# Softmax of both attentions: the inverse sum goes into the turning product instead of into the exponentials

## The chip, the cores and the metric

One NeuronCore of a Trainium2 chip runs the whole kernel. The metric is the device time of one execution in microseconds; lower is better. The kernel before has a median of 1913.64 us over three runs (1910.66 to 1914.75).

## What is computed

The reference is two layers of a hybrid backbone over 256 latent tokens and 256 context tokens of width 1024. The even layer mixes with a 2-D Fourier transform and an 8-head neighbourhood attention, then a dense SwiGLU; the odd layer has a 12-head attention with 3 key heads, an S5 recurrence, and a top-2-of-8 SwiGLU of experts. What matters here is the softmax of the two attentions, which is followed by a product with the values:

```python
s = jnp.einsum('bqhgd,bkhd->bhgqk', q_blk, k_all).astype(jnp.float32) * dh ** -0.5
p = jax.nn.softmax(s, axis=-1).astype(v_all.dtype)
return jnp.einsum('bhgqk,bkhd->bqhgd', p, v_all)
```

In the even layer latent queries see latent and context keys (512, with a bias and a mask on the latent ones) and context queries see context keys (256). In the odd layer only latent queries are used, over 512 keys. All of this is float32.

## The kernel before

The program is written by hand, engine by engine, with semaphores between them; each engine runs its own list in order. The stages follow one another: modulation and input projection of the even layer, turning of q and k, Fourier mixing, even attention (about 184 to 262 us), output product, dense layer, odd projection with S5 set-up, odd attention (about 788 to 848 us), output product, router, experts (from about 860 us to the end).

Both attentions use the same functions, one for each engine, over a list of steps: `EVEN_STEPS` has 16 (2 streams, latent then context, by 4 pairs of heads by 2 query tiles; 8 steps of 512 keys and 8 of 256), `ODD_STEPS` has 12 (6 pairs of heads by 2 query tiles, 512 keys). A step is 128 queries of two heads; the index i counts heads through both attentions, two a step, 56 in all.

For each head, in order:

- TensorE makes the scores, queries on partitions and keys along a row, into one of three PSUM banks (L681).
- DVE adds the bias in the even latent steps (L1627), which waits for POOL to have built that head's bias (`bias_ready`, POOL L2112 and L2128), and takes the negated maximum (L1632).
- ScalarE makes the exponential from PSUM into `prob[:, i % 3]` in SBUF, with the row sum beside it (L1236).
- DVE inverts the sum (L1637) and scales the exponentials by it in place (L1638).
- TensorE turns each 128x128 chunk of them into PSUM, bank 3 or 4 (L696): one transpose for each 128 keys, with the identity from the constants.
- ScalarE copies the turned chunks to `pT` in SBUF (L1246).
- TensorE multiplies them with the values, both heads of the step into bank 5 ("pv", L713).
- DVE copies that output to its place (L1646).

The order is a software pipeline that is written out. In round r TensorE issues the scores of step r, then (even layer) a modulation product of the next layer (`UNDER_ATTN`, L563), then pv of step r - 2, then the turn of step r - 1, then (odd layer) a piece of S5: output products (L940, L944), their turn (L953), the gating product (L964), and gate rows (L729). A gate row is four calls of `pe.matmul`, 128x128 by 128x128 against the identity; there are twelve rows, 48 calls. ScalarE in round r makes the exponentials of step r, then the copies of the turned chunks of step r - 1. DVE in round r makes the maxima of step r, then for each head the inverse and the scaling, then the o copy of step r - 2, then its piece of S5.

The waits that tie them: the exponential of head i waits for the turn of head i - 3 (`prob_turned`, L1235), since `prob` has three buffers; the scores of step r wait for the exponentials of step r - 1's first head (`exp_done`, L679); the turn of head i waits for its scaling (`prob_ready`, L692) and for the copy of head i - 2 (`pt_ready`, L694); pv waits for both copies (L707) and the o copy of the step before (L709).

During the even attention POOL builds the bias of the heads and tables of the odd layer's S5 in one sequence (L2112 to L2152). B is the large scratch tile of the mixing stages; in the even attention its columns 0 to 2047 held the Fourier input, and in the odd one its columns 3840 to 4863 held the S5 input `un`, which has been stored to memory by then.

Of the kernel before, what the change touches and what calls it, by code (L numbers as in the profile page):

```python
# [26 lines left out]
P = 128  # L27
# [119 lines left out]
def build(nc, a, out):  # L147
    ctx = ExitStack()
    with ctx:
        def sb(name, shape, dt=F32):  # L150
            return ctx.enter_context(nc.sbuf_tensor(name, shape, dt))

        def sem(name):
            return ctx.enter_context(nc.semaphore(name))

        bank = [ctx.enter_context(nc.psum_tensor(f"bank{i}", [P, 512], F32)) for i in range(8)]
# [9 lines left out]
        with ExitStack() as mixing:  # L166
            def mix(name, shape, dt=F32):
                return mixing.enter_context(nc.sbuf_tensor(name, shape, dt))
# [3 lines left out]
            B = mix("B", [P, FC * TOK])  # L172
# [33 lines left out]
        rinv = sb("rinv", [P, 4])  # L206

        ident = cst[:, C_ID:C_ID + P]
# [21 lines left out]
        prob = S[:, 1024:2560].rearrange("p (b n) -> p b n", b=3)  # L230
# [55 lines left out]
        def w_et(u, c):  # L286
# [30 lines left out]
        row_max, exp_done, prob_ready, prob_turned, pt_ready, o_psum, o_ready = (  # L317
            sem("row_max"), sem("exp_done"), sem("prob_ready"), sem("prob_turned"),
            sem("pt_ready"), sem("o_psum"), sem("o_ready"))
# [110 lines left out]

        qT, kT = hT[:, 0:4], hT[:, 4:8]

        def mod_bank(g):
            return bank[(0, 3, 7)[g]]

# [8 lines left out]
        def even_steps():  # L444
            steps = []
            for s in range(2):
                for p in range(NA_HEADS // 2):
                    for t in range(2):
                        q = [qT[x, p, (2 * s + t) * P:(2 * s + t + 1) * P] for x in HALVES2]
                        k = [kT[x, p, SEQ * s:] for x in HALVES2]  # L450
                        v = [[hn[:, 3, c, h * HD:(h + 1) * HD] for c in range(2 * s, 4)] for h in (2 * p, 2 * p + 1)]
                        steps.append((q, k, TOK - SEQ * s, v, p, s, t))
            return steps

        EVEN_STEPS = even_steps()
# [95 lines left out]
        def _(pe):  # L551
            def modulation(s):

                wait_slot(pe, S_MOD[s])
                g = [s < hi for _, hi in MOD_GROUPS].index(True)
                lo, hi = MOD_GROUPS[g]
                o = mod_bank(g)
                at = 30 - 2 * (s - lo)
                w = slot(S_MOD[s]).rearrange("p (k n) -> p k n", k=DC)
                for i in range(2):  # L560
                    for j in range(4):
                        c = 4 * i + j
                        mm = pe.matmul(o[32 * j:32 * j + 32, :], silc[:, c, at:at + 32], w[:, c, :],  # L563
                                       start=(s == lo and i == 0), stop=(s == hi - 1 and i == 1))
                mm.then_inc(mod_psum, 1)
# [105 lines left out]
            def attention(steps, j0):  # L671

                n = len(steps)
                for r in range(n + 2):
                    if r < n:
                        q, k, keys = steps[r][0:3]
                        i = 2 * (j0 + r)
                        if i >= 2:
                            pe.wait_ge(exp_done, i - 1)  # L679
                        for h in range(2):  # L680
                            pe.matmul(bank[(i + h) % 3][:, 0:keys], q[h], k[h], start=True, stop=True).then_inc(scores[h], 1)  # L681
                        if steps is EVEN_STEPS:
                            if r in UNDER_ATTN:
                                modulation(UNDER_ATTN[r])
                            if r == 0:
                                pe.wait_ge(four_o, 8)
                    if r >= 2:
                        pe_pv(steps[r - 2], j0 + r - 2)
                    if 1 <= r <= n:
                        for h in range(2):  # L690
                            i = 2 * (j0 + r - 1) + h
                            pe.wait_ge(prob_ready, i + 1)  # L692
                            if i >= 2:
                                pe.wait_ge(pt_ready, i - 1)  # L694
                            for c in range(steps[r - 1][2] // P):
                                mm = pe.transpose(bank[3 + i % 2][:, c * P:(c + 1) * P],  # L696
                                                  prob[:, i % 3, c * P:(c + 1) * P], ident)
                            mm.then_inc(prob_turned, 1)
                        if steps is EVEN_STEPS and r == ROW_AT + 1:
                            modulation_turn(2)  # L700
                    if steps is ODD_STEPS:
                        s5_step(r)

            def pe_pv(step, k):

                keys, v = step[2:4]
                pe.wait_ge(pt_ready, 2 * k + 2)  # L707
                if k >= 1:
                    pe.wait_ge(o_ready, k)  # L709
                o = bank[5][:, P * (k % 2):P * (k % 2) + P]  # L710
                for c in range(keys // P):
                    for h in range(2):
                        mm = pe.matmul(o[HALVES2[h], :], v[h][c], pT[:, k % 2, h, c * P:(c + 1) * P],  # L713
                                       start=(c == 0), stop=(c == keys // P - 1))
                        if c == keys // P - 1:
                            mm.then_inc(o_psum, 1)
# [277 lines left out]
            for t in range(2):  # L994
                for c in range(DC):
                    mm = pe.matmul(bank[2][:, 8 * t:8 * t + 8], hT[:, c, t * P:(t + 1) * P],
                                   vec[:, V_RW + 8 * c:V_RW + 8 * c + 8], start=(c == 0), stop=(c == DC - 1))
# [4 lines left out]
            for o, parts in ((0, [(tri, 0)]), (8, [(one, 0), (tri, 1)]), (16, [(one, 0), (one, 1)])):  # L1002
                for k, (m, t) in enumerate(parts):
                    mm = pe.matmul(bank[3][:, o:o + 8], m, sel[:, 8 * t:8 * t + 8], start=(k == 0),
                                   stop=(k == len(parts) - 1))
# [453 lines left out]
        def _(dve):  # L1459
            steps = [0]  # L1460
# [155 lines left out]
            def attention(steps, j0, oTv, c0):  # L1616
                n = len(steps)
                for r in range(n + 2):
                    if r < n:
                        keys, _, p, s, t = steps[r][2:7]  # L1620
                        for h in range(2):
                            i = 2 * (j0 + r) + h
                            sc = bank[i % 3]
                            dve.wait_ge(scores[h], j0 + r + 1)
                            if steps is EVEN_STEPS and s == 0:
                                dve.wait_ge(bias_ready, 2 * p + h + 1)
                                dve.tensor_tensor(sc[:, 0:SEQ], sc[:, 0:SEQ], bias[(2 * p + h) % 4][:, t * SEQ:(t + 1) * SEQ],  # L1627
                                                  ALU.add).then_inc(bias_used, 1)
                                dve.wait_ge(bias_used, i + 1)
                            if i >= 4:  # L1630
                                dve.wait_ge(exp_done, i - 3)
                            dve.tensor_reduce(nmax[:, i % 4:i % 4 + 1], sc[:, 0:keys], AX, ALU.max,  # L1632
                                              negate=True).then_inc(row_max, 1)
                        for h in range(2):
                            i = 2 * (j0 + r) + h
                            dve.wait_ge(exp_done, i + 1)
                            step(dve.reciprocal(rinv[:, i % 4:i % 4 + 1], rsum[:, i % 4:i % 4 + 1]))  # L1637
                            dve.tensor_scalar(prob[:, i % 3, 0:keys], prob[:, i % 3, 0:keys], rinv[:, i % 4:i % 4 + 1],  # L1638
                                              None, ALU.mult).then_inc(prob_ready, 1)
                        if steps is EVEN_STEPS and r == ROW_AT:  # L1640
                            modulation_row(2)
                    if r >= 2:
                        k = j0 + r - 2
                        p, s, t = steps[r - 2][4:7]
                        dve.wait_ge(o_psum, 2 * k + 2)
                        dve.tensor_copy(oTv[:, c0 + p, s * SEQ + t * P:s * SEQ + (t + 1) * P],  # L1646
                                        bank[5][:, P * (k % 2):P * (k % 2) + P]).then_inc(o_ready, 1)
                    if steps is ODD_STEPS:
                        s5_step(r)
# [24 lines left out]
            for u, what in enumerate(F_ORDER):  # L1674
                if u + AHEAD < F_UNITS:
                    split(u + AHEAD)
                if what[0] == "up" and what[2] == 1:
# [7 lines left out]
                    for f in range(2):  # L1685
                        c = (2 * n + f) % max(FG)
# [641 lines left out]
```

## Time and profile before

| | |
|---|---|
| Median of three runs | 1913.64 us (1910.66 to 1914.75) |
| The profiled execution | 1914.57 us, span 1912.7 us |
| Mean granted TensorE clock | 0.977 of full |
| TensorE busy | 1814.9 us, 95% |
| DVE, ScalarE, POOL busy | 66%, 52%, 16% |
| The chain that ended last | 90% TensorE, 3% DMA, 3% DVE, 2% POOL |
| DVE scaling L1638, 56 of them | 28.0 us for 40 of 512 columns, 8.0 us for 16 of 256 |
| TensorE turn L696, 192 records | 29.4 us |

The span is the time from the first to the last instruction of one profiled execution; the execution's own time is a little longer. A busy share is an average over stages with different limits, so the table says where time is spent and not what an edit is worth. A group of the timeline, such as eight matmul records, is given with its start and its length from the first start to the last end; matmul records overlap, since each lasts about 0.27 us from issue to landing while the next follows sooner.

### The profile page before, as it was taken

How to read it: one execution, taken by the hardware profiler on the slowest of the kernel's cores; microseconds unless marked ns; L12 is line 12 of the kernel's file. 1: busy time of each engine (PE TensorE's matmuls, PEld its weight loads, DVE VectorE, ACT ScalarE, POOL GpSimd, SP SyncE). 2: the span in 40 equal slices, each digit the busy share in tenths (PEclk: the TensorE clock that was granted, in tenths of full speed). 3: DMA queues.
4: the chain of work that ended last, by engine and by line, in shares of the span. 5: the costliest groups of instructions: out<-in, count | busy, mean ns of one | idle time of the engine just before them, and what ended most of it. 6: DMA issues, size and time to landing. Idle time of an engine off the chain costs nothing.

```text
span 1912.7 us, 25247 instructions
## 1 busy us (share of the span) xinstructions
PE 1814.9 (95%) x8938; PEld 1413.6 (74%) x8938; DVE 1265.6 (66%) x1329; ACT 1003.7 (52%) x1096; POOL 312.3 (16%) x584
## 2 busy tenths in 40 slices
PE   4999788999999989797999999999999999999998
PEld 2666444888888876465888888888888888888886
DVE  3243734442433234744998989989889898898997
ACT  3222423421312121363677767777777777776774
POOL 6887931011111124101000000000000000000000
PEclk8999899999999999897999999999999999999999
DMA  9788532122323151502799999999989999898994
GB/s 371 307 337 272 195 127 88 43 111 77 121 77 121 45 203 56 165 2 88 289 370 355 352 370 337 368 352 355 371 344 359 349 358 368 346 362 345 364 367 182
DMA packets 72374, 481.55 MB, mean 252 GB/s; under 512 B 8368, under 2 KB 11568, under 8 KB 17456
## 3 DMA queue, kind: packets, MB, share of 16 engines
q1 hardware_dynamic: 68720, 470.82, 64.5%
q0 software_dynamic: 2448, 7.61, 1.5%
q10 hardware_dynamic: 1136, 2.21, 0.4%
q8 instruction: 41, 0.67, 0.1%
q14 instruction: 29, 0.24, 0.0%
HBM read 473.29 MB, written 7.32 MB: 251 GB/s over the span
## 4 chain that ended last, share of the span: by engine, by line
PE 90%; DMA 3%; DVE 3%; POOL 2%; issue 1%; ACT 1%; SPq 0%; DVEq 0%; ACTq 0%; POOLq 0%
PE bank L1042 32%; PE bank L1056 16%; PE bank L775 12%; PE bank L745 4%; PE bank L804 3%; PE bank L792 3%; PE bank L625 3%; PE bank L840 2%; DMA ring<-in_ev_mod 2%; PE bank L563 2%; PE bank L1015 2%; PE bank L1025 1%; PE bank L713 1%; PE bank L605 1%; PE bank L696 1%
## 5 line engine op out<-in xcount | busy, mean ns | idle before, releaser
L1806 DVE TENSOR_TENSOR rest<-ring,WR 128x2048 fp32r<-128x2048 f32 x336 | 758.3, 2288 | 80.6 <-ACT WR L1373 80.1
L1373 ACT ACTIVATE WR<-ring 128x2048 fp32r<-128x2048 f32 x336 | 632.3, 1917 | 48.4 <-DMA ring<-in_experts 47.9
L1042 PE MATMUL bank<-WR,xer 128*128 128x512 f32 x1792 | 582.0, 397 | 0.8 <-DVE s5v L1967 0.8
L1042 PEld LDWEIGHTS bank<-WR,xer 128*128 128x128 f32 x1792 | 337.0, 188 | 70.3 <-issue 0.8
L1042 PE MATMUL bank<-rest,xer 128*128 128x512 f32 x896 | 349.5, 390 | 0.0
L1056 PE MATMUL bank<-WR,heTr 128*128 128x512 f32 x896 | 282.2, 392 | 0.0
L775 PE MATMUL bank<-hTr,WR 128*128 128x512 f32 x672 | 207.2, 390 | 0.0
L1056 PEld LDWEIGHTS bank<-WR,heTr 128*128 128x128 f32 x896 | 168.2, 188 | 34.6
L1042 PEld LDWEIGHTS bank<-rest,xer 128*128 128x128 f32 x896 | 169.1, 189 | 32.9
L1056 PE MATMUL bank<-rest,heTr 128*128 128x512 f32 x448 | 174.4, 389 | 0.0
L1658 DVE TENSOR_TENSOR rest<-ring,WR 128x2048 fp32r<-128x2048 f32 (+2 forms) x38 | 80.3, 2115 | 123.9 <-ACT WR L1298 123.6
L2232 POOL CAST gTe<-B 128x256 fp32r x8 | 3.2, 401 | 972.3 <-PE bank L1015 972.3
L775 PEld LDWEIGHTS bank<-hTr,WR 128*128 128x128 f32 x672 | 125.8, 188 | 25.9
L775 PE MATMUL bank<-hTr,rest 128*128 128x512 f32 x336 | 130.7, 389 | 0.0
L1394 ACT ACTIVATE sile<-bank 128x256 f32<-128x256 f32 x112 | 43.0, 384 | 161.5 <-PE bank L1042 161.5
L2008 POOL TENSOR_TENSOR X<-X,tmpf 128x512 f32<-128x512 f32 x32 | 52.6, 1671 | 321.0 <-DVE tmpf L1544 321.0
L1056 PEld LDWEIGHTS bank<-rest,heTr 128*128 128x128 f32 x448 | 84.2, 188 | 16.8
L1298 ACT ACTIVATE WR<-ring 128x2048 fp32r<-128x2048 f32 (+2 forms) x38 | 63.9, 1688 | 43.7 <-DMA ring<-in_ffn_up 43.7
L745 PE MATMUL bank<-ring,B 128*128 128x512 f32 x192 | 85.4, 602 | 0.9 <-issue 0.5
L563 PE MATMUL bank<-ring,rows 128*32 128x512 f32 x384 | 50.7, 648 | 25.1 <-DMA ring<-in_ev_mod 24.8
L775 PEld LDWEIGHTS bank<-hTr,rest 128*128 128x128 f32 x336 | 63.1, 188 | 13.2
L745 PEld LDWEIGHTS bank<-ring,B 128*128 128x128 f32 x192 | 36.6, 194 | 45.1 <-issue 44.3
(338 smaller groups left out, 2175.4 us busy)
## 6 DMA issues: line engine op xcount, KB each, us to landing
ring<-in_experts SPq DMA_DIRECT2D x336, 1024.0 KB, 4.8
ring<-in_ev_mod SPq DMA_DIRECT2D x24, 1024.0 KB, 9.0
ring<-in_od_mod SPq DMA_DIRECT2D x24, 1024.0 KB, 8.6
ring<-in_ffn_up SPq DMA_DIRECT2D x22, 1024.0 KB, 6.8
ring<-in_ffn_down SPq DMA_DIRECT2D x12, 768.0 KB, 5.1
ring<-in_ev_in SPq DMA_DIRECT2D x8, 1024.0 KB, 6.7
ring<-in_ev_out SPq DMA_DIRECT2D x4, 1024.0 KB, 8.5
ring<-in_od_out SPq DMA_DIRECT2D x4, 1024.0 KB, 13.5
```

What stands on the lines that cost most here:

```text
L563: mm = pe.matmul(o[32 * j:32 * j + 32, :], silc[:, c, at:at + 32], w[:, c, :], start=(s == lo and i == 0), stop=(s == hi - 1 and i == 1))
L625: mm = pe.matmul(bank[IN_BANK[j % 4]][:, :], h[i], w[k], start=(c == 0 and y == 0), stop=(c == DC - 1 and y == 2))
L745: mm = pe.matmul(bank[3 + b % 4][:, :], oTv[:, c, t * P:(t + 1) * P], w[:, c, :], start=(c == 0), stop=(c == DC - 1))
L775: mm = pe.matmul(bank[2 * m + f][:, :], w[i][:, c, f * P:(f + 1) * P], hTr[:, j, c, :], start=(c == 0 and x == 0), stop=(c == DC - 1 and x ...
L792: mm = pe.matmul(bank[t][:, :], gTr[:, i, c, t * P:(t + 1) * P], both[j][c // ks][:, c % ks, :], start=(c == 0 and x == 0), stop=(c == FG[ ...
L804: mm = pe.matmul(bank[t + 4][:, :], gTr[:, i, c, t * P:(t + 1) * P], w[j][:, k, :], start=(c == 0 and x == 0), stop=(c == FG[q] - 1 and x ...
L1042: mm = pe.matmul(bank[m % 2][:, :], xer[:, i, 4 * kh + k, :], w[j][:, 512 * k:512 * k + 512], start=(kh == 0 and k == 0 and x == 0), stop= ...
L1056: mm = pe.matmul(bank[4 + h][:, :], heTr[:, i, c, :], w[j][:, D * k + 512 * h:D * k + 512 * h + 512], start=(c == 0 and x == 0), stop=(c = ...
L1298: act.activation(part(0, h, n), ring[:, h % HALVES, 0:n], ACT.Copy).then_inc(split_hi, 1)
L1373: act.activation(part(0, h), ring[:, h % HALVES, :], ACT.Copy).then_inc(split_hi, 1)
L1658: dve.tensor_tensor(part(1, h, n), ring[:, h % HALVES, 0:n], part(0, h, n).bitcast(F32), ALU.subtract).then_inc(split_lo, 1)
L1806: dve.tensor_tensor(part(1, h), ring[:, h % HALVES, :], part(0, h).bitcast(F32), ALU.subtract).then_inc(split_lo, 1)
```

## The change

DVE no longer scales the exponentials. It writes the identity, scaled row by row by the inverse sums, into a 128x128 tile, one of three in turn; these stand in B at columns 0 to 383 in the even attention and 3840 to 4223 in the odd one. TensorE turns the unscaled exponentials by a product with that tile, so that turning and scaling are one product. DVE waits, before it writes the tile of head i, for the turn of head i - 3.

```diff
         qT, kT = hT[:, 0:4], hT[:, 4:8]
 
+        def inverse(steps, i):
+            return (B[:, P * (i % 3):P * (i % 3) + P] if steps is EVEN_STEPS else
+                    B[:, 3840 + P * (i % 3):3840 + P * (i % 3) + P])
+
...
                             for c in range(steps[r - 1][2] // P):
-                                mm = pe.transpose(bank[3 + i % 2][:, c * P:(c + 1) * P],
-                                                  prob[:, i % 3, c * P:(c + 1) * P], ident)
+                                mm = pe.matmul(bank[3 + i % 2][:, c * P:(c + 1) * P],
+                                               prob[:, i % 3, c * P:(c + 1) * P], inverse(steps, i),
+                                               start=True, stop=True)
                             mm.then_inc(prob_turned, 1)
...
                             step(dve.reciprocal(rinv[:, i % 4:i % 4 + 1], rsum[:, i % 4:i % 4 + 1]))
-                            dve.tensor_scalar(prob[:, i % 3, 0:keys], prob[:, i % 3, 0:keys], rinv[:, i % 4:i % 4 + 1],
+                            if i >= 3:
+                                dve.wait_ge(prob_turned, i - 2)
+                            dve.tensor_scalar(inverse(steps, i), ident, rinv[:, i % 4:i % 4 + 1],
                                               None, ALU.mult).then_inc(prob_ready, 1)
```

## Rows read from the trace of the kernel before

**Rows 1.** The page: TensorE's busy time, and the clock line of 40 slices.

```profile
PE 1814.9 (95%) x8938; PEld 1413.6 (74%) x8938; DVE 1265.6 (66%) x1329; ACT 1003.7 (52%) x1096; POOL 312.3 (16%) x584
...
PEclk8999899999999999897999999999999999999999
```

**Rows 2.** Groups by line and form, TensorE: the turn and the gate rows.

```profile
L696 PE MATMUL bank<-cst,S 128*128 128x128 f32 x192 | 29.4, 295 | 3.7 <-DVE S L1638 3.7
...
L729 PE MATMUL bank<-cst,mod 128*128 128x128 f32 x96 | 12.6, 275 | 0.0
```

**Rows 3.** Timeline of the odd loop: start us, us, engine, line, instruction [idle before].

```profile
810.10 1.09 PE L713 MATMUL bank<-S,B 128*64 128x128 f32 x16 [0.44 <-ACT S L1246]
...
811.12 1.09 PE L696 MATMUL bank<-cst,S 128*128 128x128 f32 x8
...
811.88 0.69 ACT L1236 ACTIVATE S<-bank,nmax 128x512 f32<-128x512 f32 x1 [0.51 <-PE bank L696]
...
812.56 1.07 ACT L1246 ACTIVATE S<-bank 128x512 f32<-128x512 f32 x2
...
812.89 0.49 DVE L1638 TENSOR_SCALAR S<-S,rinv 128x512 f32<-128x512 f32 x1
...
813.72 1.09 PE L713 MATMUL bank<-S,B 128*64 128x128 f32 x16 [0.45 <-ACT S L1246]
...
814.75 1.09 PE L696 MATMUL bank<-cst,S 128*128 128x128 f32 x8
```

**Rows 4.** Chain that ended last, odd attention: start us, us, what.

```profile
822.18 1.06 PE bank L681 x4
...
824.27 1.02 PE bank L696 x8
```

**Rows 5.** Timeline of the even attention.

```profile
211.73 1.09 PE L713 MATMUL bank<-S,B 128*64 128x128 f32 x16 [2.42 <-DVE B L1646]
...
225.09 0.43 DVE L1627 TENSOR_TENSOR bank<-bank,S 128x256 f32<-128x256 f32 x1 [4.46 <-POOL S L2128]
...
228.12 1.98 PE L713 MATMUL bank<-S,B 128*64 128x128 f32 x16 [4.33 <-ACT S L1246]
...
230.02 1.79 PE L696 MATMUL bank<-cst,S 128*128 128x128 f32 x8
```

**Rows 6.** Timeline, late odd attention: a gate row, and pv(10).

```profile
836.88 1.05 PE L729 MATMUL bank<-cst,mod 128*128 128x128 f32 x8
...
843.20 1.09 PE L713 MATMUL bank<-S,B 128*64 128x128 f32 x16 [1.26 <-ACT S L1246]
```

**Rows 7.** DVE's scaling and reciprocal: ns min/median/max, first and last start.

```profile
L1638 DVE TENSOR_SCALAR S<-S,rinv x56: 353/486/4169, 188.0 to 842.4; 128x512 f32<-128x512 f32 x40, 128x256 f32<-128x256 f32 x16
...
L1637 DVE RECIPROCAL rinv<-rsum x56: 152/164/167, 187.8 to 842.2; 128x1 f32<-128x1 f32 x56
```

**Rows 8.** Timeline, start of the odd attention, TensorE.

```profile
794.85 1.97 PE L696 MATMUL bank<-cst,S 128*128 128x128 f32 x8
...
796.74 1.79 PE L681 MATMUL bank<-HT 64*128 64x512 f32 x4
...
802.51 1.09 PE L713 MATMUL bank<-S,B 128*64 128x128 f32 x16 [0.55 <-ACT S L1246]
```

**Rows 9.** Windows: us, busy (x) PE PEld DVE ACT POOL, PEclk, DMA share, GB/s.

```profile
250.00:255.00 5.00, 3.69 (x32) 2.33 (x32) 3.59 (x14) 2.94 (x11) 1.94 (x3) 1.00 0.62 254
...
797.00:800.00 3.00, 3.00 (x25) 1.61 (x26) 2.93 (x9) 1.16 (x5) 0.00 (x0) 0.81 1.03 429
```

**Rows 10.** Chain that ended last, end of the even attention and output product.

```profile
253.84 0.38 PE bank L696 x2
...
259.20 1.06 PE bank L696 x4
...
262.25 8.80 PE bank L745 x16
...
271.95 6.87 PE bank L745 x16
```

## The prediction

> **What bounds the kernel now.** I began with the page's busy shares and its clock line [rows 1]: TensorE is busy 95% of the span and its granted clock dips only here and there. So whatever is added to TensorE costs time unless it falls into one of its waits, and DVE, which the change relieves, must be shown to be late somewhere before its saving counts. Then I read the instructions grouped by line and form [rows 2], the timelines of both attentions for who waits for whom, and the chain that ended last through them. The reader is to see three things.
>
> First, in the middle of the odd attention the loop runs TensorE, ScalarE, TensorE. The pv products of one step start at 810.10 and of the next at 813.72, a period of 3.62 us [rows 3]. The turn starts at 811.12, the exponential of the second head is released by it at 811.88, the two copies out of PSUM follow at 812.56, and they release pv. DVE's scaling of that step's second head starts at 812.89 and takes 0.49 us, so it is done at 813.38, while the turn starts at 814.75: 1.4 us of slack.
>
> Second, from 818 to 838 us (turns 6 to 9, counting from 0) TensorE hardly waits: the S5 products fill its gaps. There scores hold 1.06 us of the chain, a turn 1.02 [rows 4]; pv takes 1.03 from its start to the turn's [rows 3].
>
> Third, the even attention up to 225 us waits for POOL: the bias of one of the last heads arrives late and DVE stands idle 4.46 us for it [rows 5].
>
> **What a product costs beside a transpose.** A product of two float32 tiles is two passes of TensorE here, a transpose is one. The counts show it: the code calls transpose 192 times in the turns (96 in each attention) and the trace has 192 records; the gate rows call matmul 48 times, 128x128 by 128x128 against the identity as the new turn does, and the trace has 96 [rows 2]. A pass lasts about the same either way (means 275 and 295 ns, the latter with cold ones). Eight passes of the gate form take 1.05 us [rows 6], of which the last is its own 275 ns, so they follow each other every 0.111 us; sixteen take 15 x 0.111 + 0.275 = 1.94 us, against 1.09 for the eight transposes of a turn [rows 3]. The addition is 0.85 by that; bounds 0.8 and 1.0 (eight more passes at the chain's 1.02). I take **+0.9 us for a turn of 512 keys, +0.45 for one of 256**.
>
> The Trainium skill (TensorE: Matmul & The Clock Gate, Terms) says that transpose mode is four times faster for float32. The counts above show half of that; what four would give is rival D.
>
> **What DVE saves.** The scaling takes 486 ns over 512 columns (x40) and 353 over 256 (x16) where nothing disturbs it [rows 7]. The new operation writes 128 columns; no row has that size. Carried on from 512 and 256 it is 0.29 us; the bounds are 0.16, as the 128x1 reciprocal beside it takes [rows 7], and 0.35. I take 0.29: 0.2 us less x40 and 0.06 less x16, 9 us of DVE in all. In the odd attention it is all slack (1.4 us above) and I count it at nothing; if that cover went, it would gain its 0.2 a head. The added wait of DVE asks for the turn of three heads back, for which the exponential that DVE has just waited for has itself waited: zero, at most some 0.05 us a head. Behind it on DVE stand the o copy and the next maxima, for which pv and the exponentials wait. Nothing else moves: no DMA and no POOL instruction is added, and SP's queue is as it was.
>
> **Odd attention, step by step.**
> - Turn 0 is at the low clock, 1.97 us for its eight [rows 8], so sixteen add 1.9 and end at 798.7. The scores behind it took 1.79 cold; now they start as the clock rises (it is 0.81 over 797 to 800 [rows 9]) and take some 1.2. Then pv 1.0, turn 1 at 800.9 with 1.9, scores 1.05, and pv(1) at 803.85 where it was at 802.51 [rows 8]: **+1.35** (0.6 to 2.2 by when the clock rises).
> - The loop: TensorE's own sum becomes 1.06 + 1.03 + 1.9 = 4.0, and ScalarE's path grows by the first head's half, 0.4, to 4.0 too. Three periods of 3.62 become 4.0, +1.15, and the one before them, 3.97 already for DVE's S5 work, adds 0.05: **+1.2**.
> - Turns 6 to 8 stand in the stretch without a wait: 3 x 0.9 = **+2.7**.
> - Turns 9 and 10: here ScalarE with its table loads is later than TensorE; pv(10) waits 1.26 us for it [rows 6]. Turn 9 reaches it through the first head, +0.4, turn 10 by what its end overshoots, +0.2. Turn 11 is at the end of TensorE's own queue, +0.9: **+1.5**.
>
> Sum +6.75.
>
> **Even attention.**
> - Up to 225 us five turns of 512 keys add 4.5 us to TensorE. They fall into its waits (2.42 us at 211.73 alone) and behind POOL's bias, for which DVE waits 4.46 us [rows 5]. I count **0**; if POOL gave up that cover, each would cost its 0.9.
> - Steps 5 and 6. TensorE sat idle 4.33 us until 228.12, then worked at the low clock: pv 1.98, turn 1.79 [rows 5]. Now turn 5 and its scores end near 226.0 and the gap is 2.1 us. The gap of 2.42 us at 211.73 was followed by pv in 1.09, the full clock; that is the nearest row, so I take pv at 1.0 and the turn at 1.9, 2.9 for what took 3.6, and +0.45 through turn 7's first head: -0.3, counted as **0**. At the low clock it would be +2.15.
> - Seven steps of 256 keys go round pv, the first head's two transposes, exponential, reciprocal, scaling, o copy, pv (the two hold 0.38 us of the chain [rows 10]). They become four passes, +0.22; the scaling gives back 0.06: 7 x 0.16, **+1.1**. Here alone DVE is on the path.
> - The last turn, 1.06 us of the chain for four at the low clock [rows 10], has nothing beside it: 0.45 more at the full clock, 0.9 at the low one; **+0.8**.
>
> Sum +1.9, of both attentions **+8.65 us**. What comes behind each (output product, dense layer, experts) starts from its last o copy and is bound by itself as before, so the shift goes through. The profiled execution took 1914.57 us (span 1912.7), and would take 1923.2. It stands 0.93 above the median of the three runs, 1913.64; from the median the forecast is **1922.3 us**. The bounds of the parts (start 0.6 to 2.2, steps 5 and 6 -0.3 to 2.15, the turn 0.8 or 1.0, DVE's wait) give 1919 to 1927.5 for this case.
>
> **Rivals.**
> - **B, the clock pays it back.** The new passes fill gaps and the clock falls less. Place: the end of the even attention with the start of the output product, and the start of the odd attention. Price: the output product's first sixteen took 8.80 us, its second sixteen 6.87 [rows 10], 1.9; the turn ahead of it half of its 1.06 and the pvs around it about as much, 1.1; turn 0 of the odd attention with sixteen passes at 1.94 instead of 3.9, 2.0. Together 5.0: 1917.3, within 0.2%. For it: the clock stayed full over 250 to 255 us with transposes in every step [rows 9], and more work can only help. Against it: the wait that precedes the last turns is ScalarE's and DVE's and stays, and ahead of the odd turn 0 nothing is added. Chance 0.12.
>  The Trainium skill (TensorE: Matmul & The Clock Gate, Part 4) says that transposes do not count as busy for the clock gate; by that rule exchanging them would help the most. The full clock of 250 to 255 us doesn't speak for it.
> - **C, DVE is what is late.** Faster. Place: every turn for whose scaling TensorE is ready before DVE; price: the whole 9 us, with the new passes inside TensorE's waits: 1904.6. It decides as soon as most turns wait for DVE. For it: the loop of 256 keys runs through DVE. Against: 1.4 us of slack in the odd loop, and 20 us in which TensorE waits for nobody. Chance 0.05.
> - **D, the product costs four times the transpose.** A turn would take 4.1 us, +3. Odd: start 4.5, loop 4 x 2.5, turns 6 to 8 9, the last three 8; even: 15 before 225 less some 6 of cover, then 5.5, 7 and 1.5. Together 54: 1968. Against it stand the 96 records for 48 calls. Chance 0.03.
> - **E, it doesn't do what it says:** the product goes out as one pass. Then TensorE is as before and DVE's share is worth 1 us at most: 1913. Chance 0.04.
>
> **How the numbers follow.** About 0.2% (3.8 us) is what a measurement of this kernel can tell from no change. The forecast has 0.76, of which 0.02 could end within it. Slower: 0.74 + 0.03 = 0.77. Within: 0.12 + 0.04 + 0.02 = 0.18. Faster 0.05. The range holds the forecast's own 1919 to 1927.5 and reaches down to B and up to a leak of 2.5 us from the cover before 225: 1916.5 to 1930.
>
> **What the profile would show.** The turn's line with 384 records of the same mean and 1.9 us a turn; DVE's line with 56 of about 0.29 us; in the odd loop pv every 4.0 us; no wait for DVE before a turn there; DVE's wait for POOL near 225 us shorter by some 1.5 us but still there; the pv behind it at 1.09 instead of 1.98. The forecast is wrong if the turn's records stay 192, if the dips of the clock at 258 and 788 us are gone, or if DVE's wait for POOL is.

## The result, and the profile after

The changed kernel takes **1919.28 us** (median of 8 runs, 1917.62 to 1921.58) where the kernel before took 1911.04 (8 runs, 1908.79 to 1914.75): ratio 1.004, 95% interval 1.003 to 1.005, so 8.2 us more by the medians. Forecast were 8.65 us more and 1922.3 us; that time stood on a median of 1913.64 us from three runs, which is 2.6 us above that of the eight. The profiled execution took 1920.99 us, its span is 1919.2.

Its groups by line and form, the turn's products (two passes each) and DVE's tile, answer to [rows 2, 7]; the columns are as there, busy us and mean ns:

```profile
L700 PE MATMUL bank<-B,S 128*128 128x128 f32 x384 | 54.4, 297 | 0.0
L700 PEld LDWEIGHTS bank<-B,S 128*128 128x128 f32 x384 | 49.0, 206 | 7.0 <-issue 4.7 <-DVE B L1645 2.3
...
L1645 DVE TENSOR_SCALAR B<-cst,rinv 128x128 f32<-128x128 f32 x56 | 21.6, 385 | 2.2 <-DVE rinv L1642 0.3
```

Twice the records at the same mean, 54.4 us of TensorE where it was 29.4. DVE's line fell from 36.0 to 21.6 us; undisturbed it takes 0.29 us, as the timeline shows.

The odd loop in the timeline of the changed kernel, to be read beside [rows 3]:

```profile
808.00 1.09 PE L718 MATMUL bank<-S,B 128*64 128x128 f32 x16
...
809.02 2.05 PE L700 MATMUL bank<-B,S 128*128 128x128 f32 x16
...
810.28 0.69 ACT L1241 ACTIVATE S<-bank,nmax 128x512 f32<-128x512 f32 x1 [0.70 <-PE bank L700]
...
810.96 1.07 ACT L1251 ACTIVATE S<-bank 128x512 f32<-128x512 f32 x2
811.00 0.30 PEld L685 LDWEIGHTS bank<-HT 64*128 64x128 f32 x4
811.00 1.13 PE L685 MATMUL bank<-HT 64*128 64x512 f32 x4
...
811.29 0.29 DVE L1645 TENSOR_SCALAR B<-cst,rinv 128x128 f32<-128x128 f32 x1
...
812.08 0.85 PEld L718 LDWEIGHTS bank<-S,B 128*64 128x64 f32 x16 [0.78 <-ACT S L1251]
812.08 1.09 PE L718 MATMUL bank<-S,B 128*64 128x128 f32 x16
```

The turn fills 809.02 to 811.00, the scores 811.00 to 812.08, and pv follows at once: TensorE has no wait left, and the period is 4.08 us instead of 3.62. The exponential of the second head now starts 1.26 us behind the turn's start (809.02 to 810.28), where it was 0.76: it waits for twice the passes. DVE's tile is ready at 811.58, 1.5 us before the next turn starts at 813.11.

Where the time came from, by the stages' first and last instructions in the two profiled executions:

| stage | before | after | difference | forecast |
|---|---|---|---|---|
| start to the even attention's first scores | 184.47 | 183.65 | -0.8 | 0 |
| even attention, to the output product | 77.78 | 80.58 | +2.8 | +1.9 |
| output product, dense layer, odd projection | 526.95 | 525.99 | -1.0 | 0 |
| odd attention, to the output product | 58.50 | 64.99 | +6.5 | +6.75 |
| output product, router, experts | 1065.00 | 1063.99 | -1.0 | 0 |

The differences add up to the spans' 6.5 us. This compares one execution with one, and how much of it is the change is read from the profiled executions of the experiments below. The odd attention is steady: with plain transposes in it 58.48 and 58.49 us (the change, and later its one-pass form, in the even attention alone), with the change in it 65.65 and 64.99 (the odd attention alone, and without the added wait). The even attention is not: with plain transposes it lasted 77.78, 76.03 and 75.92 us, with the change 80.58, 79.58 and 76.82. The last stage, which the change does not touch, lasted from 1059.9 to 1065.0 us, the first took from 183.2 to 186.2. So the traces show +6.5 to +7.2 for the odd attention, and the even one's +2.8 to no better than some 2 us.

The even attention in the timeline of the changed kernel, beside [rows 5]:

```profile
208.57 0.43 DVE L1632 TENSOR_TENSOR bank<-bank,S 128x256 f32<-128x256 f32 x1 [5.04 <-POOL S L2135]
...
223.86 0.43 DVE L1632 TENSOR_TENSOR bank<-bank,S 128x256 f32<-128x256 f32 x1 [4.18 <-POOL S L2135]
...
226.86 1.18 PE L718 MATMUL bank<-S,B 128*64 128x128 f32 x16 [2.45 <-ACT S L1251]
...
227.96 3.56 PE L700 MATMUL bank<-B,S 128*128 128x128 f32 x16
```

DVE waits for POOL's bias twice now, 5.04 and 4.18 us, where it was once, 4.46. In this pair of executions the added passes before 225 us cost nothing, as forecast. But the turn behind it took 3.56 us; the granted clock over 228.0 to 231.5 us was 0.55, most of it the low level.

The loop of 256 keys in the chain that ended last of the changed kernel, beside [rows 10]:

```profile
255.28 0.66 PE bank L718 x8
255.94 0.66 PE bank L700 x4
...
257.06 0.20 ACT S L1241
257.28 0.17 DVE rinv L1642
...
257.68 0.29 DVE B L1653
...
258.11 0.66 PE bank L718 x8
...
264.23 7.13 PE bank L750 x16
```

The first head's turn holds 0.66 us of the chain (four passes) where it held 0.38 (two transposes), and the period is 2.83 us where pv stood at 253.18 and 255.80 before, 2.62. The output product's first sixteen records took 7.13 us instead of 8.80: the granted clock over 258 to 262 us was 1.00 where it was 0.60.

### The profile page after: what moved, and what is told of

Same layout as the page of the kernel before. It is cut to its first block, busy times and chain, and to the rows that moved or that the text cites. A ratio compares the mean times of both kernels' runs of the same rounds, so it can differ in the third digit from the quotient of the medians.

```text
span 1919.2 us, 25684 instructions
## 1 busy us (share of the span) xinstructions
PE 1833.9 (96%) x9130; PEld 1440.2 (75%) x9130; DVE 1250.9 (65%) x1329; ACT 1005.3 (52%) x1096; POOL 310.9 (16%) x584
## 4 chain that ended last, share of the span: by engine, by line
PE 90%; DMA 4%; DVE 2%; POOL 2%; issue 1%; ACT 1%; SPq 0%; DVEq 0%; ACTq 0%; POOLq 0%
PE bank L1047 32%; PE bank L1061 16%; PE bank L780 12%; PE bank L750 4%; PE bank L809 3%; PE bank L797 3%; PE bank L629 3%; PE bank L845 2%; DMA ring<-in_ev_mod 2%; PE bank L567 2%; PE bank L1020 2%; PE bank L700 2%; PE bank L1030 1%; PE bank L718 1%; PE bank L609 1%
## 5 line engine op out<-in xcount | busy, mean ns | idle before, releaser
L750 PEld LDWEIGHTS bank<-ring,B 128*128 128x128 f32 x192 | 35.9, 190 | 43.9 <-issue 43.2
```

The source lines that it names most:

```text
L750: mm = pe.matmul(bank[3 + b % 4][:, :], oTv[:, c, t * P:(t + 1) * P], w[:, c, :], start=(c == 0), stop=(c == DC - 1))
```

## The experiments

Theory P: what the change costs is the second pass of TensorE that a product of float32 tiles takes and a transpose doesn't. Rivals: W, DVE's added wait and tile; F, the form of the product (its weight load lasts 190 ns against 140) whatever the passes; H, only products keep the clock up; C, DVE's saving is worth something. All ratios are to the kernel before in runs on the same chip: its median was 1911.47 us (17 runs) beside the product alone, each transpose twice and one attention at a time; 1911.15 (31) beside the one-pass product in both attentions, the kernel without the added wait and the two with the o copy moved; 1910.75 (20) beside the one-pass product in one attention.

**The product alone.** The kernel before, with one edit:

```diff
-                                mm = pe.transpose(bank[3 + i % 2][:, c * P:(c + 1) * P],
-                                                  prob[:, i % 3, c * P:(c + 1) * P], ident)
+                                mm = pe.matmul(bank[3 + i % 2][:, c * P:(c + 1) * P],
+                                               prob[:, i % 3, c * P:(c + 1) * P], ident,
+                                               start=True, stop=True)
```

> The product with the plain identity in place of the transpose; DVE scales the exponentials in place as before, and the added wait and the tile are not there. Theory P (the change's cost is the second pass of each float32 product on TensorE): 7 to 11 us above the kernel before, so the same as the full change or up to 1.5 us above it, because DVE's saving is not there; 384 records of the turn, the odd loop with a pv every 4.1 us. Rival W (the cost is on DVE's side, the added wait or the tile's write): within 2 us of the kernel before.

Measured: 1919.37 us (6 runs), ratio 1.0052, interval 1.0039 to 1.0064. That is the whole cost with neither the tile nor the wait, so W falls: it said within 2 us of the kernel before. Its loop of 256 keys takes 2.89 us a step (pv at 253.44 and 256.33), 0.06 more than the change's 2.83: that is DVE's saving there, as forecast. In its odd loop pv stands every 4.12 us (805.21, 809.34, 813.46), 0.04 more than the change's.

**Each transpose twice.** The kernel before, the call repeated into the same place:

```diff
                                 mm = pe.transpose(bank[3 + i % 2][:, c * P:(c + 1) * P],
                                                   prob[:, i % 3, c * P:(c + 1) * P], ident)
+                                mm = pe.transpose(bank[3 + i % 2][:, c * P:(c + 1) * P],
+                                                  prob[:, i % 3, c * P:(c + 1) * P], ident)
```

> The kernel before with each transpose of the turn issued twice into the same place: as many passes as the products have (384 records), all in transpose mode. Theory P (the number of passes): the same as the product alone within 1.5 us, sixteen records a turn in about 2.0 to 2.1 us, a pv every 4.1 us in the odd loop. Rival F (it is the product's form, its longer weight load of 190 against 140 ns): at least 3 us below the product alone. Rival H (only products keep the clock up, transposes do not count for it): the end of the even attention and the output product's first sixteen records are as slow as before (8.8 us), where they took 7.1 with the change; under P with the gap filled either way they take about 7.1.

Measured: 1917.61 us (6 runs), ratio 1.0043, interval 1.0029 to 1.0056. Its groups by line and form:

```profile
L696 PE MATMUL bank<-cst,S 128*128 128x128 f32 x192 | 47.2, 289 | 3.2 <-DVE S L1640 3.2
L698 PE MATMUL bank<-cst,S 128*128 128x128 f32 x192 | 45.4, 280 | 0.0
L698 PEld LDWEIGHTS bank<-cst,S 128*128 128x128 f32 x192 | 28.0, 146 | 0.0
```

(The busy times of the two interleaved lines overlap.) As many passes with the short weight load cost nearly the same: pv every 4.06 us in the odd loop (804.95, 809.00, 813.06). It is the pass count. Theory P had said the same as the product alone within 1.5 us, and the medians differ by 1.76, a little more; the two intervals overlap, and rival F asked for 3 us. So the form is worth little: 0.06 us a step in the odd loop by the two traces, and on the whole time 1.76 us by the medians, which is not told from none. For H, the sign named ahead turned out to decide nothing: the first sixteen took 7.13 us here, but they took that also in three kernels whose even attention has plain transposes, each issued once (below). What speaks against H is the clock itself, in the window of the even attention's end (us from start to end: span, busy (x) of TensorE, weight loads, DVE, ScalarE and POOL, granted clock, DMA share, GB/s):

```profile
240.00:262.00 22.00, 16.54 (x148) 11.96 (x149) 14.75 (x47) 11.60 (x42) 10.41 (x16) 1.00 0.61 252
```

Doubled transposes held it at 1.00, as the two-pass products did, where the kernel before shows 0.93. That is one execution each; the mean clocks of all runs, further below, say the same.

**One attention at a time.** In `pe` and `dve` the old and the new lines stand under a condition:

```diff
+                                if steps is EVEN_STEPS:
...
+                                else:
+                                    mm = pe.transpose(bank[3 + i % 2][:, c * P:(c + 1) * P],
+                                                      prob[:, i % 3, c * P:(c + 1) * P], ident)
```

> The change in the even attention alone, the odd one as before. Theory P with the traces read: the even attention 2.8 us longer, the output product behind it 1.7 us shorter because the clock does not dip, together +0.5 to +2 us. Rival C (DVE's saving is worth something here): below the kernel before.

Measured: 1912.72 us (11 runs), ratio 1.0008, interval 0.9999 to 1.0017: +1.5 us by the ratio, as expected, at the edge of what can be told from none.

> The change in the odd attention alone, the even one as before. Theory P: +5.5 to +7.5 us, nearly all of the change's cost, and this plus the run with the even attention alone adds up to the whole. Rival W (the added wait and the tile): half of it at each attention, as each has half of the turns.

Measured: 1918.8 us (5 runs), ratio 1.0049, interval 1.0036 to 1.0062; its odd attention lasts 65.65 us against 58.50. By the medians that is +7.3 us, inside the expected 5.5 to 7.5, and with the even attention's 1.2 it adds up to 8.6; by the ratios it is +9.4, above the range, and the two make 10.9 against the change's 8.2, a gap that these intervals allow. The odd attention carries nearly all, though each has half of the turns' work: in the even one POOL's bias hides it up to 225 us. One row of this kernel, whose even attention is untouched, mattered beyond its purpose; from its chain:

```profile
262.18 7.13 PE bank L754 x16
```

The output product ran at the full clock here as well, with plain transposes ahead of it, and so it did, in 7.13 us, in the kernels with the one-pass product in the odd attention alone and with the o copy moved up. The 8.80 us of the kernel before were one execution's, so the 1.7 us that this stage won cannot be put down to the change.

**The product in one pass.** The exponentials and the tile are written as float32r, through a view of the same memory, with the rest of the change as it is:

```diff
-        prob = S[:, 1024:2560].rearrange("p (b n) -> p b n", b=3)
+        prob = mixr[:, 1024:2560].rearrange("p (b n) -> p b n", b=3)
...
-            return (B[:, P * (i % 3):P * (i % 3) + P] if steps is EVEN_STEPS else
-                    B[:, 3840 + P * (i % 3):3840 + P * (i % 3) + P])
+            at = 6656 + 4096 + (0 if steps is EVEN_STEPS else 3840) + P * (i % 3)
+            return mixr[:, at:at + P]
```

> The change with the exponentials and the scaled tile written as float32r, a shorter mantissa, so that the product of the turn goes out as one pass; the attention probabilities are rounded by it. Theory P (the second pass is the cost): 192 records again and the time of the kernel before within 2 us, a pv every 3.6 us in the odd loop, though product, tile and added wait are all there. Rival F (the product's form) or W (the wait and the tile): +5 us or more, as with the change.

Measured: 1916.59 us (12 runs), ratio 1.0029, interval 1.0019 to 1.0039. **A miss**: P said within 2 us, and it was 5.4. The passes did halve and the odd loop was back to 3.6 us, but look at the even attention. Windows of 240 to 262 us: span, TensorE busy, weight loads, DVE, ScalarE, POOL, granted clock, DMA. First this kernel:

```profile
240.00:262.00 22.00, 19.44 (x110) 13.63 (x110) 13.88 (x45) 10.08 (x36) 7.53 (x9) 0.58 0.57 240
```

and the kernel before:

```profile
240.00:262.00 22.00, 14.42 (x122) 9.49 (x120) 15.07 (x48) 11.31 (x40) 11.55 (x18) 0.93 0.62 258
```

The clock is at its low level for most of the stretch (0.50 over 250 to 262 us), and TensorE is busy 19.4 us for what took 14.4. Two more kernels were made to tell whether that was chance, with the one-pass product in one attention only (the same edit, under the condition above).

> The one-pass float32r product, the tile and the added wait in the odd attention alone; the even one is as in the kernel before. Theory P (the second pass is what the change costs, and the 5 us that the one-pass product still cost in both attentions are the low clock in the even one's loop of 256 keys): within 1.5 us of the kernel before, mean clock 0.975 to 0.979, a pv every 3.6 us. Rival F (a product in place of a transpose costs even in one pass): +2.5 us or more, since 12 of the 28 steps and the whole loop bound by TensorE are here.

Measured: 1909.55 us (12 runs), ratio 0.9993, interval 0.9983 to 1.0003. The product, the tile and the wait, in one pass, cost nothing that can be measured in the very loop that carries the change's cost. From its timeline:

```profile
806.93 1.09 PE L727 MATMUL bank<-S,B 128*64 128x128 f32 x16 [0.40 <-ACT S L1260]
...
810.52 1.09 PE L727 MATMUL bank<-S,B 128*64 128x128 f32 x16 [0.40 <-ACT S L1260]
```

3.59 us a step, and pv waits for ScalarE again. F and W fall, and the second pass is left.

> The same in the even attention alone. Theory P with the clock: +3 to +6 us, mean clock 0.968 to 0.972, the stretch from 240 to 262 us at a granted clock near 0.5 to 0.7 where the kernel before has 1.00. If the low clock of the one look was chance: within 1.5 us of the kernel before and the mean clock as there.

Measured: 1916.93 us (8 runs), ratio 1.0031, interval 1.0021 to 1.0042. The low clock is no chance. Its mean clock was 0.969 to 0.972 in all 8 runs, and 0.968 to 0.972 in the 12 of the kernel with both; the kernel before had 0.973 to 0.980 in the 51 runs beside them, the one-pass product in the odd attention 0.975 to 0.978. Its window and its loop of 256 keys:

```profile
240.00:262.00 22.00, 19.67 (x116) 13.52 (x112) 14.73 (x45) 10.53 (x39) 9.78 (x16) 0.63 0.69 287
```

```profile
253.27 1.12 PE L727 MATMUL bank<-S,B 128*64 128x128 f32 x8
254.32 1.12 PE L706 MATMUL bank<-mixr 128*128 128x128 f32 x4
255.37 1.23 PE L690 MATMUL bank<-HT 64*128 64x256 f32 x4
256.54 1.12 PE L727 MATMUL bank<-S,B 128*64 128x128 f32 x8
```

pv, turn and scores take 1.12, 1.12 and 1.23 us where they took 0.66, 0.66 and 0.70, and a step 3.27 us instead of 2.62. Over the last three steps that is 1.9 us; the even attention as a whole lasts 82.40 us against 77.78, +4.6 of the +5.9 of the ratio.

The kernel before is not the only measure of this window. In the kernel just above, with the one-pass product in the odd attention alone, the even attention has plain transposes, and its clock fell too:

```profile
240.00:262.00 22.00, 15.86 (x114) 10.15 (x114) 14.61 (x49) 10.15 (x37) 8.88 (x14) 0.84 0.52 218
```

The profiled executions of the kernels with one plain transpose for each 128 keys here show 0.93, 0.84, 0.84 and 1.00; those of the six kernels with two passes, products or transposes, show 1.00 each; those of the two with the one-pass product 0.58 and 0.63. So the low clock also comes without the product, for a shorter stretch, and the mean clocks of all 20 runs are what shows that the one-pass product makes it last. It is not the tile or the wait, which the even attention of the change has too, with 1.00. What in the one-pass product lets the clock fall further than a transpose of the same shape and record length, these runs do not tell.

**Without the added wait.**

```diff
-                            if i >= 3:
-                                dve.wait_ge(prob_turned, i - 2)
                             dve.tensor_scalar(inverse(steps, i), ident, rinv[:, i % 4:i % 4 + 1],
```

> The change without the wait that it adds on DVE (the exponential before it has waited for the same turn). Theory P: the time of the change within 1 us, +7 to +9. Rival W: 3 us or more below the change.

Measured: 1917.37 us (8 runs), ratio 1.0037, interval 1.0024 to 1.0050: +7.1 us by the ratio, +6.2 by the medians, where the change has 8.2 with an interval of 1.003 to 1.005. The two are not told apart, so no cost of the wait shows; the times alone would leave room for about 3 us, and it is the product alone, as dear as the change without any wait, that closes it.

**DVE's o copy moved up.** The loop of 256 keys runs through the o copy only because DVE's list puts it behind the second head's scaling:

```diff
                         for h in range(2):
                             i = 2 * (j0 + r) + h
+                            if h == 1 and r >= 2:
+                                o_copy(r)
                             dve.wait_ge(exp_done, i + 1)
...
-                    if r >= 2:
-                        k = j0 + r - 2
...
+                    if r >= n:
+                        o_copy(r)
```

> The kernel before with DVE's o copy moved up, between the two heads' scalings of the same round. If DVE is on the path in the loop of 256 keys by the order of its work (pv waits for the o copy, which stands behind the second head's exponential), that loop goes from 2.6 to about 2.4 us a step, 1 to 2.5 us in all; the odd loop, which waits for ScalarE, stays at 3.6. If DVE is not on the path anywhere: no difference.

Measured: 1909.13 us (12 runs) against 1911.15, ratio 0.9990, interval 0.9979 to 1.0000. From its timeline:

```profile
249.94 0.28 DVE L1623 COPY B<-bank 128x128 f32<-128x128 f32 x1
250.14 0.15 DVE L1647 RECIPROCAL rinv<-rsum 128x1 f32<-128x1 f32 x1
...
250.50 0.66 PE L713 MATMUL bank<-S,B 128*64 128x128 f32 x8 [0.30 <-ACT S L1246]
...
252.79 0.66 PE L713 MATMUL bank<-S,B 128*64 128x128 f32 x8 [0.41 <-ACT S L1246]
```

pv waits for ScalarE's copies now, and a step takes 2.29 us. Of the kernels without float32r it has the lowest median, below both kernels of this case; its interval ends at 1.0000, so that it is faster than the kernel before is just short of certain.

> The same move in the changed kernel. In the loop of 256 keys, 2.83 us a step now, pv no longer waits for the o copy; I expect about 2.5 and 1 to 2.5 us less than the change. If it gains more here than in the kernel before, DVE's order and not the pass is a part of the change's cost.

Measured: 1917.48 us (12 runs), ratio 1.0033, interval 1.0021 to 1.0045. A step of 256 keys takes 2.56 us (252.05, 254.61), 0.27 less than with the change alone; the kernel before won 0.33. The gain of 1 to 2.5 us that was expected against the change is not told from none (ratios 1.0033 and 1.004, intervals overlapping). With the o copy moved in both, on the same chip, the change costs 8.35 us by the medians (1909.13 and 1917.48), as without the move. The cost stays, so it isn't DVE's order.

## Why the prediction was right

The time, the sign and the mechanism were right: 1919.28 us lies in the range, and +8.2 us against +8.65. That the size came out so close is in part luck, since parts of the sum were off both ways. One of the signs that the prediction named for being wrong did occur: the clock's dip at 258 us is gone from the profiled execution, while the one at 788 us is there (0.50 over 788 to 795 us, before and after). It was a poor sign: kernels with plain transposes there lack that dip too. Point by point:

- **A product is two passes, a transpose one.** Shown: 384 records, and the transposes issued twice cost the same within the intervals. A turn's records take 2.05 us where I worked out 1.94. The gate rows' pace of 0.111 us was slightly too fast; the turn measures 0.118, with a weight load that lasts as long (192 and 190 ns), and no run tells why. From the turn's start to the next instruction it went from 1.03 to 1.98 us, so the addition is 0.95, between the bounds of 0.8 and 1.0. The figure of four of the Trainium skill (TensorE: Matmul & The Clock Gate, Terms) is not what this kernel shows; two is. Rival D is out.
- **Start of the odd attention, +1.35: mis-sized.** From the first scores to pv(1) it was 13.31 us and is 13.69, +0.4. I priced turn 0 at the low clock throughout, 3.9 us; it took 2.95, because the clock rose within it:

```profile
795.87 2.95 PE L700 MATMUL bank<-B,S 128*128 128x128 f32 x16
798.74 1.13 PE L685 MATMUL bank<-HT 64*128 64x512 f32 x4
```

  The product alone shows the same 2.95. It depends on the execution: with two-pass products here the stretch took 13.69, 13.69, 13.90, 14.04 and 14.35 us in five kernels, so +0.4 to +1.1, inside the prediction's bounds from 0.6 only in part.
- **The loop, +1.2:** +1.5 from pv(1) to pv(5); 4.08 us a step where I had 4.0, the 0.08 being the turn's. **Turns 6 to 8, +2.7:** +2.9. **Turns 9 to 11, +1.5:** +1.7 from pv(8) to the output product. Together with the start 6.5 against 6.75: the odd attention's sum came out right because a term too large and three slightly too small met.
- **Even attention up to 225 us, 0:** -0.4 to pv(5). The other executions bound this no better than by some 2 us: from the first scores to pv(5) plain transposes took 40.1 to 43.7 us and the change 42.2 to 43.2. I wrote that DVE's wait for POOL would shrink by 1.5 us, and it did not: 4.18 us for 4.46, 5.10 in the kernel with the change in the even attention alone. I had left out DVE's own long scalings, though the longest of 4169 ns stands in [rows 7]: 4.17 us at 188.90 in the kernel before, and a second of 4.08 at 207.31. The profiled execution of the change had none, so the attention ran ahead of POOL and waited for it twice. But that is not the smaller tile's doing: with the change in the even attention alone the tile took as long. First the kernel before, then that kernel, with the POOL instruction behind the start of each:

```profile
188.90 4.17 DVE L1638 TENSOR_SCALAR S<-S,rinv 128x512 f32<-128x512 f32 x1
189.62 1.28 POOL L2128 TENSOR_TENSOR S<-B,cst 128x512 f32<-128x512 f32 x1
```

```profile
188.51 3.97 DVE L1650 TENSOR_SCALAR B<-cst,rinv 128x128 f32<-128x128 f32 x1
189.22 1.28 POOL L2143 TENSOR_TENSOR S<-B,cst 128x512 f32<-128x512 f32 x1
```

  In the profiled execution of the change that tile was done at 188.36, before the same POOL instruction started at 188.81.

- **Steps 5 and 6, 0 (bounds -0.3 and +2.15):** +1.3 between pv(5) and pv(7). The gap shrank to 2.45 us (I had 2.1) and pv ran at 1.18, but the clock fell behind it and the turn took 3.56. The step that failed was to read from one gap of 2.42 us that another would do no harm.
- **256 keys and the last turn, +1.9:** +2.0, and as a sum that is luck. From pv(7) to pv(14), the seven steps, it was +2.5 where I had 1.1; from pv(14) to the output product it was -0.5 where I had +0.8, because the kernel before had its low clock there and the change did not. What is the change's is steadier. A step rose by 0.20 to 0.22, with 0.27 for the passes (2.89 in the product alone against 2.62) and 0.06 back from DVE, against the 0.22 and 0.06 of the prediction; seven of these are 1.5 us. And at the full clock on both sides the end takes 3.30 us against 2.85 (the kernel with the change in the odd attention alone), the 0.45 that I had for a turn of 256 at the full clock. The rest of the +2.5 lies in the first steps, which vary from one execution to the next: the seven took 23.36 us in that same kernel with plain transposes, and 23.12 in the change.
- **Rival C, DVE:** its saving is 0.06 us a step of 256 keys and, by the two odd loops of 4.12 and 4.08 us, 0.04 there; the time of the product alone is not told apart from the change's.
- **Rival B, the clock pays it back:** in part. The profiled execution regained 1.7 us behind the even attention, but three kernels with plain transposes there did the same. More passes do make the full clock regular at the end of the even attention, 1.00 in six profiled executions of six against one of four. The mean clock is somewhat higher with more passes: 0.981 to 0.982 in the 6 runs of the product alone and 0.978 to 0.982 with each transpose twice, 0.975 to 0.979 in the 17 of the kernel before beside them. How much time that gave back isn't isolated. By the rule of the Trainium skill (TensorE: Matmul & The Clock Gate, Part 4) that transposes do not count as busy for the clock in the same way, doubling them should leave it where it was; it rose about as with products, so these runs speak against it.

## What to carry to other kernels

Count the records that each call leaves before pricing it: folding a scale into a transpose turned one pass of TensorE into two here for float32, which could pay only where the engine that is relieved ends the wait and TensorE has room. Here the relieved engine had 1.4 us of slack in the loop that mattered, and what bound the short loop was the place of a copy in its list, which moving one instruction took away. And compare a stage over several kernels whose code is the same there before giving its difference to an edit: two executions of such a stage differed here by up to 5 us.

## What was not expected of the hardware

- A one-pass float32r product of 128 columns in place of a transpose, of about the same record length (277 and 273 ns in the middle), went with a granted clock of 0.58 and 0.63 over 240 to 262 us, where four profiled executions with the transpose show 0.84 to 1.00, and brought the mean clock below every run of the kernel before beside it (0.968 to 0.972 against 0.973 to 0.980). With two passes the window was at 1.00 in all six kernels.
- DVE's scaling beside a busy POOL: over 128x512, 0.49 us undisturbed, it took 4.17 us, and the 128x128 tile, 0.29 us undisturbed, took 3.97 to 3.99 us in the same place in three kernels (the change in the even attention alone, without the added wait, and with the o copy moved). The smaller size does not shorten it much. In each of these POOL began a run of instructions about 0.7 us or less behind DVE's start and kept on until it ended; why DVE's instruction is held, no run tells.
